# Encoder step: final transposes, copies and stores moved in among the products of the last feed-forward chunk

## What is computed

```python
def swiglu(h, w_gate, w_up, w_down):
    return (jax.nn.silu(h @ w_gate) * (h @ w_up)) @ w_down
...
        h = rms_norm(x, g_ffn[i]) * (1.0 + scale2) + shift2
        x = x + gate2 * swiglu(h, w_gate[i], w_up[i], w_down[i])
    return x, ...
```

## Time and profile before

| | |
|---|---|
| time, median of 3 executions (lowest to highest) | 3534.0 us (3533.2 to 3535.52) |
| time of the profiled execution | 3515.84 us |
| its span, first to last instruction | 3514.1 us |
| mean granted TensorE clock in it | 0.975 of full speed |

### The profile page before, as it was taken

One profiled execution on the slowest core, in us unless ns is written; L12 is line 12 of the kernel. 1 busy time (PEld: TensorE's weight loads), 2 busy tenths in 40 slices (PEclk: granted clock), 3 DMA queues, 4 the chain that ended last, 5 costly groups with the idle time before them and its releaser, 6 DMA issues.

```text
span 3514.1 us, 48640 instructions
## 1 busy us (share of the span) xinstructions
PE 3305.1 (94%) x20417; PEld 2983.4 (85%) x20417; DVE 2087.6 (59%) x1756; ACT 1339.6 (38%) x1018; POOL 140.9 (4%) x141
## 2 busy tenths in 40 slices
PE   7999997777979999999999999777999999999998
PEld 4677775555969999999999999657999999999998
DVE  4487883445787777666777667775444443344443
ACT  3344444555344433444333443324222232322321
POOL 0000000000000000000000000010000000000000
PEclk9999999999989999999999999888999999999999
DMA  9776765776646555565555655453334333333331
GB/s 354 264 271 235 259 240 196 264 256 238 218 141 211 196 191 182 177 212 192 191 186 177 210 191 191 146 190 120 132 119 131 126 125 130 120 131 120 131 123 56
DMA packets 325245, 645.15 MB, mean 184 GB/s; under 512 B 11561, under 2 KB 14129, under 8 KB 324401
## 3 DMA queue, kind: packets, MB, share of 16 engines
q1 hardware_dynamic: 317984, 630.29, 52.2%
q10 hardware_dynamic: 7194, 13.91, 1.1%
HBM read 630.47 MB, written 13.69 MB: 183 GB/s over the span
## 4 chain that ended last, share of the span: by engine, by line
PE 86%; DVE 5%; DMA 4%; ACT 3%; issue 2%; SPq 0%; POOL 0%; ACTq 0%; DVEq 0%; POOLq 0%
PE bank L1410 23%; PE bank L1412 22%; PE bank L1411 22%; PE bank L1487 3%; PE bank L1437 3%; PE bank L1489 3%; PE bank L1488 3%; DMA raw<-in_w_ada 3%; DVE sq_sum L967 1%; PE bank L1446 1%; PE bank L1617 1%; PE bank L1422 1%; PE bank L1589 1%; ACT e_buf L738 0%; PE bank L1618 0%
## 5 line engine op out<-in xcount | busy, mean ns | idle before, releaser
L924 DVE TENSOR_TENSOR w_lo<-raw,w_hi 128x2048 fp32r<-128x2048 f32 x324 | 741.5, 2291 | 912.7 <-ACT w_hi L557 912.7
L557 ACT ACTIVATE w_hi<-raw 128x2048 fp32r<-128x2048 f32 x324 | 618.4, 1915 | 1391.0 <-PE bank L1412 1200.8
L1410 PE MATMUL bank<-h_hi,w_hi 128*128 128x384 f32 x3136 | 1062.7, 339 | 44.5 <-DVE h_lo L990 31.7
L1412 PE MATMUL bank<-h_hi,w_lo 128*128 128x384 f32 x3136 | 1052.0, 335 | 0.0
L1411 PE MATMUL bank<-h_lo,w_hi 128*128 128x384 f32 x3136 | 1050.9, 335 | 0.0
L1410 PEld LDWEIGHTS bank<-h_hi,w_hi 128*128 128x128 f32 x3136 | 591.1, 189 | 89.5 <-issue 83.6
L1411 PEld LDWEIGHTS bank<-h_lo,w_hi 128*128 128x128 f32 x3136 | 591.4, 189 | 0.0
L1412 PEld LDWEIGHTS bank<-h_hi,w_lo 128*128 128x128 f32 x3136 | 590.9, 188 | 0.0
L1410 PE MATMUL bank<-act_hi,w_hi 128*128 128x384 f32 x1408 | 472.7, 336 | 0.0
L1412 PE MATMUL bank<-act_hi,w_lo 128*128 128x384 f32 x1408 | 470.5, 334 | 0.0
L1411 PE MATMUL bank<-act_lo,w_hi 128*128 128x384 f32 x1408 | 470.5, 334 | 0.0
(11 more groups left out here) (203 smaller groups left out, 2558.3 us busy)
## 6 DMA issues: line engine op xcount, KB each, us to landing
raw<-in_w_ada SPq DMA_DIRECT2D x192, 1024.0 KB, 5.6
raw<-in_w_gate SPq DMA_DIRECT2D x88, 1024.0 KB, 5.2
raw<-in_w_up SPq DMA_DIRECT2D x88, 1024.0 KB, 5.2
raw<-in_w_down SPq DMA_DIRECT2D x88, 1024.0 KB, 5.0
raw<-in_w_qkv SPq DMA_DIRECT2D x40, 1024.0 KB, 5.2
raw<-in_cache_k SPq DMA_DIRECT2D x32, 1024.0 KB, 5.5
raw<-in_cache_v SPq DMA_DIRECT2D x32, 1024.0 KB, 6.4
raw<-in_w_o SPq DMA_DIRECT2D x16, 1024.0 KB, 5.0
```

The source lines that it names most:

```text
L557: act.activation(w_hi[:, s], raw[:, s], ACT.Copy).then_inc(hi_ready, 1)
L924: dve.tensor_tensor(w_lo[:, s], raw[:, s], w_hi[:, s].bitcast(f32), ALU.subtract).then_inc(lo_ready, 1)
L1410: pe.matmul(out, w, a, start=start, stop=False)
L1412: return pe.matmul(out, wl, a, start=False, stop=stop)
```

## The change

PE's loop now has 10 rounds, and the last chunk is written out behind it with `last=True`. In it the products of quarters 1, 2 and 3 are each interrupted at k == 2, half-way through the block, by the 12 transposes of the quarter before (`turn_rows`), and quarter 3 is turned at the end. The transposes of quarter q go to the first three banks of the four from which it has just been added (`y_bank(q)` = `down_bank(q)`, plus t). Before the products of quarters 2 and 3 PE waits for the copies out of those banks (`y_act`, `y_dve`). DVE does its two copies of a quarter (t = 0, 2) right behind that quarter's add, ACT its one (t = 1) behind its last weight block. SP issues 12 stores of 256 KB (128 rows of 512 columns), in the order of quarters and tiles, each after its own copy. The count of transposes (48), copies (12) and stored bytes stays.

```diff
@@ -282,6 +282,9 @@
 
             return W + n // 4, n % 4
 
+        def y_bank(q):
+            return down_bank(q)
+
         def down_bank(s):
 
             return 4 if s % 2 == 0 else 0
@@ -463,13 +466,17 @@
                 load_cols(W, w_gate[1], c * 512)
                 load_cols(W + 1, w_up[1], c * 512)
                 load_down(W + 2, 1, c)
+            for q in range(4):
+                cols = slice(512 * q, 512 * q + 512)
+                for t in range(TT):
+                    if t == 1:
+                        sp.wait_ge(y_act, q + 1)
+                    else:
+                        sp.wait_ge(y_dve, 2 * q + t // 2 + 1)
+                    dst = y_prompt[0, t * P:(t + 1) * P] if t < 2 else y_sample.rearrange("b t n -> (b t) n")
+                    sp.dma_start(dst[:, cols], yrow[:, t, cols]).then_inc(y_stored, 16)
             sp.wait_ge(pool_stored, 16 * 9 * 8)
-            sp.wait_ge(y_act, 6)
-            sp.wait_ge(y_dve, 6)
-            for t in range(TT):
-                dst = y_prompt[0, t * P:(t + 1) * P] if t < 2 else y_sample.rearrange("b t n -> (b t) n")
-                sp.dma_start(dst, yrow[:, t]).then_inc(y_stored, 16)
-            sp.wait_ge(y_stored, 16 * TT)
+            sp.wait_ge(y_stored, 16 * 4 * TT)
 
 
 
@@ -903,10 +910,9 @@
                 dense_chunk(W_FFN1 + c * 3, c + CHUNKS)
             dense_chunk(W_FFN1 + 3 * (CHUNKS - 1), 2 * CHUNKS - 1, last=True)
 
-            for i in range(1, 12, 2):
-                t, q = i % TT, i // TT
-                act.wait_ge(yT_done, i + 1)
-                act.activation(yrow[:, t, q * 512:(q + 1) * 512], bank[:, i % 6], ACT.Copy).then_inc(y_act, 1)
+            for q in range(4):
+                act.wait_ge(yT_done, TT * q + 2)
+                act.activation(yrow[:, 1, q * 512:(q + 1) * 512], bank[:, y_bank(q) + 1], ACT.Copy).then_inc(y_act, 1)
 
 
 
@@ -1309,6 +1315,12 @@
                     down_add(4 * W + 17 + s, s, r, layer)
                     following(W, 20 + s)
 
+            def rows_out(q):
+
+                for t in (0, 2):
+                    dve.wait_ge(yT_done, TT * q + t + 1)
+                    dve.tensor_copy(yrow[:, t, q * 512:(q + 1) * 512], bank[:, y_bank(q) + t]).then_inc(y_dve, 1)
+
             def dense_chunk(W, c, r, last=False):
 
                 for n in range(4, 11):
@@ -1319,6 +1331,8 @@
                     if not last:
                         dense(W, 12 + s)
                     down_add(4 * W + 9 + s, s, r, 1)
+                    if last:
+                        rows_out(s)
 
             with loop(dve, 0, CHUNKS - 1, {step: 4 * ADD}) as c:
                 mixed_chunk(W_FFN0 + c * 5, c, ADA_FFN + c * 2, 0, R_FFN0 + c * 4, mixed)
@@ -1395,11 +1409,6 @@
                 dense_chunk(W_FFN1 + c * 3, c + CHUNKS, R_FFN1 + c * 4)
             dense_chunk(W_FFN1 + 3 * (CHUNKS - 1), 2 * CHUNKS - 1, R_FFN1 + 4 * (CHUNKS - 1), last=True)
 
-            for i in range(0, 12, 2):
-                t, q = i % TT, i // TT
-                dve.wait_ge(yT_done, i + 1)
-                dve.tensor_copy(yrow[:, t, q * 512:(q + 1) * 512], bank[:, i % 6]).then_inc(y_dve, 1)
-
 
 
 
@@ -1453,11 +1462,13 @@
                     last = pe.matmul(bank[:, stat_bank, 0:TOK], ones[:], sq_sum[:, g], start=(g == 0), stop=(g == 3))
                 last.then_inc(sq_used, 1)
 
-            def to_features(W, n, b0, act_h, act_l, k0, start, stop):
+            def to_features(W, n, b0, act_h, act_l, k0, start, stop, rows_of=None):
 
                 W, s = unit(W, n)
                 pe.wait_ge(lo_ready, 4 * W + s + 1)
                 for k in range(4):
+                    if k == 2 and rows_of is not None:
+                        turn_rows(rows_of)
                     for m in range(4):
                         cols = slice(m * P, (m + 1) * P)
                         last = product(bank[:, b0 + m, 0:TOK], w_hi[:, s, k, cols], w_lo[:, s, k, cols],
@@ -1717,12 +1728,15 @@
                     last = tile_features(W, n, m, 0, h_hi, h_lo, 12, False, True)
                     last.then_inc(up_tile if m < 3 else sub_used, 1)
 
-            def down_rest(W, n, r):
+            def down_rest(W, n, r, rows_between=False):
 
                 for s in range(1, 4):
                     if s >= 2:
                         pe.wait_ge(residual_taken, r + s - 1)
-                    to_features(W, n + s, down_bank(s), act_hi, act_lo, 0, True, True)
+                        if rows_between:
+                            pe.wait_ge(y_act, s - 1)
+                            pe.wait_ge(y_dve, 2 * s - 2)
+                    to_features(W, n + s, down_bank(s), act_hi, act_lo, 0, True, True, s - 1 if rows_between else None)
 
             def mixed_chunk(W, c, a, r, hr):
 
@@ -1762,7 +1776,15 @@
                 pe.wait_ge(ada_done, a + 2)
                 down_rest(W, 16, r)
 
-            def dense_chunk(W, c, r, hr):
+            def turn_rows(q):
+
+                pe.wait_ge(residual_taken, R_END - 3 + q)
+                for t in range(TT):
+                    for k in range(4):
+                        last = pe.transpose(bank[:, y_bank(q) + t, k * P:(k + 1) * P], x[:, 4 * q + k, t * P:(t + 1) * P], ident[:])
+                    last.then_inc(yT_done, 1)
+
+            def dense_chunk(W, c, r, hr, last=False):
 
                 pe.wait_ge(residual_taken, r - 1)
                 for j in range(4):
@@ -1779,10 +1801,10 @@
                     pe.wait_ge(act_ready, 4 * c + k + 1)
                     for m in range(4):
                         cols = slice(m * P, (m + 1) * P)
-                        last = product(bank[:, 4 + m, 0:TOK], w_hi[:, s, k, cols], w_lo[:, s, k, cols],
+                        done = product(bank[:, 4 + m, 0:TOK], w_hi[:, s, k, cols], w_lo[:, s, k, cols],
                                        act_hi[:, k, :], act_lo[:, k, :], k == 0, k == 3)
-                last.then_inc(sub_used, 1)
-                down_rest(W, 8, r)
+                done.then_inc(sub_used, 1)
+                down_rest(W, 8, r, last)
 
             with pe.Fori(0, CHUNKS) as c:
                 mixed_chunk(W_FFN0 + c * 5, c, ADA_FFN + c * 2, R_FFN0 + c * 4, 4)
@@ -1827,19 +1849,10 @@
             map_group(3)
             pe.wait_ge(residual_taken, R_FFN1)
             norm_stats(3)
-            with pe.Fori(0, CHUNKS) as c:
+            with pe.Fori(0, CHUNKS - 1) as c:
                 dense_chunk(W_FFN1 + c * 3, c + CHUNKS, R_FFN1 + c * 4, 8)
-
-
-            for i in range(12):
-                t, q = i % TT, i // TT
-                if i == 0:
-                    pe.wait_ge(residual_taken, R_END)
-                if i >= 6:
-                    pe.wait_ge(y_act if i % 2 else y_dve, (i - 6) // 2 + 1)
-                for k in range(4):
-                    last = pe.transpose(bank[:, i % 6, k * P:(k + 1) * P], x[:, 4 * q + k, t * P:(t + 1) * P], ident[:])
-                last.then_inc(yT_done, 1)
+            dense_chunk(W_FFN1 + 3 * (CHUNKS - 1), 2 * CHUNKS - 1, R_FFN1 + 4 * (CHUNKS - 1), 8, last=True)
+            turn_rows(3)
 
 
 INPUTS = ["x_prompt", "x_sample", "c_prompt", "c_sample", "cache_k", "cache_v", "state_pool", "w_ada",
```

## The result

The changed kernel takes 3524.4 us (median of 8 executions, 3522.1 to 3527.6) against 3533.5 us for the kernel before (8 executions, 3530.8 to 3535.5): ratio 0.9975, 95% interval 0.9964 to 0.9986, that is 9.1 us or 0.25% less.

A forecast was written before the change was run, and what follows sets the result against it. PE, with no idle time in the last chunk, was taken as the bound, leaving a 19.9 us tail; 4.1 + 3.07 + 2.86 + 0.69 + 0.06 + 2.1 + 0.4 = 13.3, gain 6.6: 3534.0 to 3527.4 us, range 3524.7 to 3531.0.

The forecast's parts named there:

- the spread of the medians: Unprofiled medians: 0.8 us allowed in the range, as the executions of before ran from 3533.2 to 3535.5.
- the insertions: Last chunk on PE: 36 transposes among the products are paid in full, 4.1 us with the changes back and forth.
- The spare times of the waits: Last chunk: adds end 0.98 us before PE needs them, copies over 3 us before; the waits cost nothing.
- Leaving the loop: PE's last chunk written out: fetching its instructions costs zero; from above, one late block might stand for 2 us.
- The tail's first gap: Behind the last product: the add of quarter 3 keeps the transposes waiting 3.07 us, as before.
- term 1: Tail: third copy begins 2.86 us after the first of the last twelve transposes, as before; lower bound 1.6.
- term 2: End of the tail: the last 256 KB store lands in 2.1 us, with ends 1.5 and 3.5.
- the offset of the profile: Unprofiled median stands 18.2 us above the profiled execution and stays so; changed span forecast at 3507.5 us.
- Full clock: Tail: the last twelve transposes stay at full clock, 1.25 us less; gain 7.8, 3526.2 us; chance 0.17.
- Late stores: Tail: last stores land late, in 3.5 or 4.0 us; gain 5.2 or 4.7, 3529 us; chance 0.10.
- The slower rival: Last chunk: clock falls at the inserted transposes and stays down; 13.5 us slower, 3547.5 us; chance 0.03.
- The "copies and stores pile up" rival: End: transposes paid on PE while stores still pile up; no gain beyond 1 us from trailing copies; chance 0.02.

The follow-up runs named there:

- extra_turns: Changed kernel with 12 more identity transposes into a free bank ahead of quarter 0's; stretch from the last chunk's branch to span's end 117.5 us, changed kernel 115.8.
- unroll_only: Kernel before with only PE's last chunk written out behind the loop; stretch from the last chunk's branch to span's end 124.5 us, before 122.9.
- turns_only: Changed kernel's transposes and copies, but the three 1 MB stores of the kernel before, issued when all copies are done; 3532.6 us, ratio 0.9994 to before.
- turns_at_k0: Changed kernel with each quarter's transposes in front of the next block (k == 0); stretch from the last chunk's branch to span's end 133.4 us, changed kernel 115.8.
- stores_only: Kernel before with SP alone changed: twelve 256 KB stores, each behind its own copy, transposes still at the end; 3528.7 us, ratio 0.9988 to before.
- before_again: Kernel before, unaltered, measured against itself; 3531.0 against 3533.3 us, ratio 0.9994.
- after_again: Changed kernel run once more, unaltered, against the kernel before; 3525.7 us, ratio 0.9977.
- turns_at_k1: Changed kernel with the transposes a quarter of a block earlier (k == 1); stretch from the last chunk's branch to span's end 119.5 us, changed kernel 115.8.
- turns_at_k3: Changed kernel with the transposes a quarter of a block later (k == 3); stretch from the last chunk's branch to span's end 115.8 us, changed kernel 115.8.
- busy_gap: Kernel before with 24 extra identity transposes on PE during the last add; stretch from the last chunk's branch to span's end 121.6 us, before 122.9.

## Why the prediction was right and wrong

The forecast, 3527.4 us, lies 3.0 above the measured 3524.4. Of these, 0.5 are the two terms below, 0.5 are the median of before, 3533.5 in eight executions where it was 3534.0 in three, and 2.0 are the spread of the medians.

**Right: what bounds it.** The last chunk on PE is full, and the insertions cost 3.96 us (4.1 forecast; extra_turns confirms the price). The spare times of the waits held: PE waited for no add and no copy among the products. Leaving the loop cost nothing (unroll_only). The tail's first gap stayed at 3.07. All nine early stores were free.

**Wrong, term 1: the last twelve transposes.** I took the 2.86 us of the trace of before, at the lower clock, and gave full clock a chance of 0.17. In all four profiles with this PE order (three of the changed kernel, and turns_only) they ran at full clock: the third copy began 1.57 us behind the first transpose. That is 1.3 us more gain. The step that failed read "the gap ahead of them does not change, so I take 2.86": the gap was the same, but in these runs the same gap came with either clock, by when it came.

**Wrong, term 2: the last store.** 2.1 us forecast, 3.0 measured; even the quickest of the twelve took 2.4. My interpolation came from the 15 KB store and a 512 KB one, and set aside the 3.5 us that rows 9 show for 256 KB behind another; the last store here, too, was issued right behind two others. The estimate of 2.6 us from "DMA: Bandwidth & Descriptors" of the Trainium skill, section "Anatomy of one DMA", which I set aside because the page describes another issuing path, was nearer than mine.

The two terms nearly cancel: 6.6 us were forecast for the stretch and 7.1 came. That is luck in part.

**Wrong, and what carried the result out of the range: the spread of the medians.** 7.1 us is 3526.4 from a median of 3533.5; the first measurement gave 3524.4. I had allowed 0.8 us for the spread, read from three single executions of before. The three medians of the changed kernel run from 3524.4 to 3526.3, and before against itself differed by 2.2. A range for one measured median had to allow 2 us on either side; the step that failed is that 0.8. The measured gains, 9.1, 7.6 and 5.7, stand around the 7.1 that the traces show.

**Wrong beside it: the offset of the profile.** I took it that the 18.2 us between the profiled execution of before and its median would stay, and forecast a span of 3507.5. It was 3525.9: the profiled execution of the changed kernel stood 3.2 us above its median. The forecast of the median doesn't rest on this; the last section shows where the 18 us lie.

**The rivals.** Full clock was the true one. Late stores came more than half-way, 0.9 us of 1.4. The slower rival, a clock that falls among the products, did not come true, because the adds stayed hidden; turns_at_k0 shows what it takes: gaps of 3 us. The "copies and stores pile up" rival is what turns_only measures, 1.2 us of gain where I had said 1. That the numbers agree is luck: I had put the 1 us down to the copies, and it was the clock.

## What to carry to other kernels

Moving work from an idle tail into a stage where its engine is full gains next to nothing by itself: 4.0 us were paid for 5.2 saved, and the rest was the clock. With the stores split it gained some 0.7 us more at equal clock, by the estimate above, and a better clock besides. The larger part was to cut the last transfer into pieces that start as their data is ready (3.3 us in stores_only, some 5 at equal clock by estimate), which needed no move of the transposes at all; a shorter chain ahead of the last piece, tile by tile, brought 2.3 more. Ask what a thing that must wait for the very last result costs, and make that piece small, before you reorder anything.

## What was not expected of the hardware

**The attention stage's time follows the clock.** Windows over the three middle rounds of its loop, in the profiled execution of before and in before_again, the same code (columns as headed):

```profile
core 0: us, PE busy (x) PEld busy (x) DVE busy (x) ACT busy (x) POOL busy (x), PEclk, DMA share, GB/s
621.10:846.70 225.60, 178.62 (x1777) 125.02 (x1778) 100.67 (x141) 131.76 (x141) 0.00 (x0) 0.98 0.70 245
```

```profile
625.20:865.10 239.90, 192.97 (x1777) 133.47 (x1778) 100.68 (x141) 131.74 (x141) 0.00 (x0) 0.91 0.65 230
```

The same instructions, 225.6 us at a granted clock of 0.98 and 239.9 at 0.91; PE's busy time is longer by just the same 14.3 us. That is 14 of the 18 us by which the profiled execution of before stood below its median, which the prediction could not explain; the other 4 lie ahead of these rounds (621.1 against 625.2). Executions in between occur too (235.4 in after_again); among 15 later executions of the kernel before, two took 3510.9 and 3515.1 us. From the last round of that stage on, all profiles agree to 0.3 us until the last chunk, so what profiles of one kernel differ by lies here and ahead of it. That the medians spread for the same reason is likely, but not shown, since other executions left no trace. Why the stage takes the one time or the other wasn't settled.

**When the clock falls in a gap.** Behind dense products it fell 2.2 to 2.4 us into the gap in before, before_again, unroll_only and stores_only, and 2.3 to 3.6 us behind the products at each of the four gaps of turns_at_k0. It did not fall at all in a gap of the same 3.07 us in the changed kernel's three profiles, turns_only, turns_at_k1 and turns_at_k3. It then stayed down for 3.4 us in before and before_again, and for 6.8 in unroll_only and stores_only. extra_turns and busy_gap show that timing and idleness decide, and that transposes keep the clock up as products do; by what rule isn't shown by these runs.
